# Decode attention in a paged-cache kernel: value products interleave two sequences, page numbers move ahead of a wait

## The reference, cut to what matters

```
sel_k, sel_v = sel_blocks(concat([cache_slc[page_table], new rows]))   # 1024 cached keys, 8 pages of 128 a sequence
win_k, win_v = concat([cache_win, new rows])                           # 512 cached keys
o_cmp = softmax(q . kcmp)  @ vcmp        # 32 compressed keys
o_slc = softmax(qr . kg)   @ vg          # cached keys, one block masked out
o_win = softmax(qr . win_k) @ win_v      # window keys
o = o_cmp * g0 + o_slc * g1 + o_win * g2
```

## Time and profile before

| what | value |
|---|---|
| median of three runs | 3044.95 us |
| profiled execution | 3043.31 us, its span 3041.5 us |
| PE busy | 2548.6 us (84% of the span) |
| DVE busy | 1624.8 us (53%) |
| ACT busy | 1039.4 us (34%) |
| mean TensorE clock granted | 0.877 of full speed |
| decode phase of layer 0 | from 395.7 to about 500 us |
| decode phase of layer 3 | from 2659.1 to about 2765 us |

### The profile page before, as it was taken

The page is one execution under the profiler, slowest core; times in us unless marked ns, Lnnn a source line. Parts: engine busy times, 40 slices in busy tenths (PEclk is TensorE's granted clock), DMA queues, the critical chain, the costliest instruction groups (busy, mean ns, idle before and its releaser), DMA issues. The chain is left out here.

```text
span 3041.5 us, 43305 instructions
## 1 busy us (share of the span) xinstructions
PE 2548.6 (84%) x16878; PEld 2276.5 (75%) x16878; DVE 1624.8 (53%) x2612; ACT 1039.4 (34%) x1839; POOL 126.0 (4%) x108
## 2 busy tenths in 40 slices
PE   6998677999693878786999975679999997678999
PEld 5886546999672778534999974569999885547998
DVE  4352634655546746177655665356565344635655
ACT  3221523544333111103544531145443212424543
POOL 0000000001000000000000013000010000000000
PEclk9798888999796989556999987679999797889999
DMA  5531553555230000001455430225545442372553
GB/s 210 198 97 52 180 187 112 164 165 163 95 126 21 1 1 1 32 14 51 162 166 166 146 118 0 83 87 167 165 161 171 166 135 88 107 249 87 166 165 115
DMA packets 109833, 360.70 MB, mean 119 GB/s; under 512 B 12868, under 2 KB 14660, under 8 KB 106180
## 3 DMA queue, kind: packets, MB, share of 16 engines
q1 hardware_dynamic: 107332, 353.79, 35.4%
q10 hardware_dynamic: 2304, 4.20, 0.4%
HBM read 345.97 MB, written 28.61 MB: 123 GB/s over the span
## 5 line engine op out<-in xcount | busy, mean ns | idle before, releaser
L322 DVE TENSOR_TENSOR low<-ring,high 128x1024 fp32r<-128x1024 f32 (+1 forms) x426 | 519.8, 1222 | 429.5 <-ACT high L315 429.1
L315 ACT ACTIVATE high<-ring 128x1024 fp32r<-128x1024 f32 (+1 forms) x426 | 448.6, 1056 | 653.0 <-PE bank L337 633.7
L336 PE MATMUL bank<-bl,high 128*128 128x288 f32 (+1 forms) x1616 | 482.2, 298 | 0.0
L335 PE MATMUL bank<-bh,high 128*128 128x288 f32 (+1 forms) x1616 | 479.6, 297 | 0.0
L337 PE MATMUL bank<-bh,low 128*128 128x288 f32 (+1 forms) x1616 | 474.0, 293 | 0.0
L336 PEld LDWEIGHTS bank<-bl,high 128*128 128x128 f32 (+1 forms) x1616 | 304.8, 189 | 0.8
L337 PEld LDWEIGHTS bank<-bh,low 128*128 128x128 f32 (+1 forms) x1616 | 304.5, 188 | 0.2
L336 PE MATMUL bank<-hidden_low,high 128*128 128x288 f32 x1024 | 304.5, 297 | 0.0
L335 PEld LDWEIGHTS bank<-bh,high 128*128 128x128 f32 (+1 forms) x1616 | 303.8, 188 | 0.8
L335 PE MATMUL bank<-hidden_high,high 128*128 128x288 f32 x1024 | 301.4, 294 | 0.0
L337 PE MATMUL bank<-hidden_high,low 128*128 128x288 f32 x1024 | 299.3, 292 | 0.0
(11 more groups left out here) (484 smaller groups left out, 4726.4 us busy)
## 6 DMA issues: line engine op xcount, KB each, us to landing
ring<-in_wts SPq DMA_DIRECT2D x428, 512.0 KB, 3.3
xp<-in_cmp SPq DMA_DIRECT2D x112, 256.0 KB, 3.0
raw<-in_slc SPq DMA_DIRECT2D x64, 256.0 KB, 3.6
shared<-in_slc SPq DMA_DIRECT2D x64, 256.0 KB, 3.6
out_win_out<-in_win SPq DMA_DIRECT2D x16, 1016.0 KB
raw<-in_winT SPq DMA_DIRECT2D x8, 1024.0 KB, 6.7
shared<-in_winT SPq DMA_DIRECT2D x8, 1024.0 KB, 6.7
w<-in_w SPq DMA_DIRECT2D x2, 2048.0 KB, 8.3
```

The costliest lines, as they stand in the source:

```text
L315: act.activation(ch.high[:, n % HIGHS, 0:w], ch.ring[:, q % SLOTS, 0:w], ACT.Copy).then_inc(ch.high_made, 1)
L322: dve.tensor_tensor(ch.low[:, q % SLOTS, 0:w], ch.ring[:, q % SLOTS, 0:w], ch.high[:, n % HIGHS, 0:w].bitcast(F32), ALU.subtract).then_inc ...
L335: pe.matmul(out, wh, src_h(k), start=(start and k == ks[0]), stop=False)
L336: pe.matmul(out, wh, src_l(k), start=False, stop=False)
```

## The change

There are two edits. In the products with the values PE goes over the tiles in the outer loop and over the two sequences in the inner one, so that two neighbouring instructions work for different sequences; the products with the new and compressed rows are ordered in the same manner. Their number and shapes stay. And `load_pair` reads all 16 page numbers of a pair into registers first, then waits for the buffer (where it must), then issues the two windows, and then the 16 pages.

```diff
-def load_pair(ch, sp, n_, dst, pt, bp):
-
+def load_pair(ch, sp, n_, dst, pt, bp, free=None):
+
+    pages = [[sp.value_load(pt[0:1, b * NPG + j:b * NPG + j + 1], min_val=0, max_val=79) for j in range(NPG)] for b in (2 * bp, 2 * bp + 1)]
+    if free is not None:
+        sp.wait_ge(*free)
     for b2 in range(2):
-        b = 2 * bp + b2
-        for j in range(NPG):
-            page = sp.value_load(pt[0:1, b * NPG + j:b * NPG + j + 1], min_val=0, max_val=79)
+        sp.dma_start(dst[:, b2, NPG:, :], ch.dram[f"winT{n_}"][2 * bp + b2]).then_inc(ch.pair_loaded[bp % 2], 16)
+    for b2 in range(2):
+        for j, page in enumerate(pages[b2]):
             sp.dma_start(dst[:, b2, j, :].unsqueeze(1), ch.dram[f"slc{n_}"][bass.ds(page, 1), :, :].rearrange("a p c -> p a c")).then_inc(ch.pair_loaded[bp % 2], 16)
-        sp.dma_start(dst[:, b2, NPG:, :], ch.dram[f"winT{n_}"][b]).then_inc(ch.pair_loaded[bp % 2], 16)
...
                     load_pair(ch, sp, n_, raw[1], pt, 1)
                     for bp in range(2, DB // 2):
-                        sp.wait_ge(s["pv_done"], bp - 1)
-                        load_pair(ch, sp, n_, raw[bp % 2], pt, bp)
+                        load_pair(ch, sp, n_, raw[bp % 2], pt, bp, (s["pv_done"], bp - 1))
...
-                        for b2, rows in seqs:
-                            for t in range(NPG, NT):
+                        for t in range(NPG, NT):
+                            for b2, rows in seqs:
                                 pe.matmul(win[rows, 0:2 * P], pT2[:, t, rows], kvp[:, b2, t, 2 * P:], start=(t == NPG), stop=False)
...
-                        for b2, rows in seqs:
-                            for t in range(NPG):
+                        for t in range(NPG):
+                            for b2, rows in seqs:
                                 pe.matmul(slc[rows, 0:2 * P], pT2[:, t, rows], kvp[:, b2, t, 2 * P:], start=(t == 0), stop=False)
                         pe.wait_ge(s["pt_copied"], 4 * bp + 4)
+                        for out, j in ((slc, 0), (win, 1)):
+                            for b2, rows in seqs:
+                                pe.matmul(out[rows, 0:2 * P], pTn[:, j, rows], vtok[0:NS, 2, 2 * j:2 * j + 2, :].rearrange("p a c -> p (a c)"), start=False, stop=True)
                         for b2, rows in seqs:
-                            for out, j in ((slc, 0), (win, 1)):
-                                pe.matmul(out[rows, 0:2 * P], pTn[:, j, rows], vtok[0:NS, 2, 2 * j:2 * j + 2, :].rearrange("p a c -> p (a c)"), start=False, stop=True)
                             mm = pe.matmul(cmp[rows, 2 * P:4 * P], pTn[:, 2, rows], vcs[:, 2 * bp + b2, :], start=True, stop=True)
```

## The result

The changed kernel took 3026.83 us, the median of five runs (3023.80 to 3029.56), against 3043.26 us for five runs of the kernel before. The ratio is 0.9944, with a 95% interval from 0.9929 to 0.9958. The forecast was 3029.0 us, with a range of 3020 to 3041. The profiled execution has a span of 3026.0 us, 15.5 less than before. The two decode phases, from PE's first product to the end of the last transpose, went from 104.7 and 105.7 us to 98.7 and 97.6: 14.1 of the 15.5 us are there. The other 1.4 us were gained ahead of the first of the two phases, where the change moves nothing but the reads for pair 0's load.

What follows compares the result with a forecast made beforehand. Decode phases were taken as bound by PE's chain of pairs and, beside it, SP's slowly issued loads. Three pairs' 3.65 us less pair 1's later start gave -8.05 and -7.85 us, together -15.9: 3029.0 us, range 3020 to 3041.

Steps and rivals of the forecast that it cites:

- pair 0's share: Pair 0's products with the values: their 3.65 us saving would vanish in PE's wait for pair 1's load.
- the rivals: Four alternatives: transfers gain nothing (0.13), transfers at 412 GB/s (0.15), PE stays at half clock (0.05), sequences don't overlap (0.05).
- The rival in which the transfers run as the program's first ones: Page and window loads at 412 GB/s, pair 1 landing 0.9 and 1.1 us late, whole 3025.0 us; chance 0.15.
- the signs: Expected in the trace: shorter products, PE waiting for pair 1 only, first DMA about 9 us later, clock back within products.
- The gain of a pair's products: Products with the values in the decode phases: 6.6 us against 10.25 at full clock, 3.65 us gained a pair.
- The estimate from the value of the Trainium skill for three column tiles: Products with the values: 1.59 times for two sequences, 8.3 us, gaining 1.95 a pair, whole 3039 us; not adopted.
- The landing of pair 1: Pair 1's load: 16 uncovered reads, then 20.2 us of transfer, starting pair 1 2.9 us later in layer 0, 3.1 in layer 3.
- Pairs 2 and 3: Their loads in the decode phases: reads covered, none late, with 3.5 us to spare.
- That the windows go first costs and gives nothing by itself: Window order in load_pair: worth nothing, because PE waits for all 18 DMAs.

Runs made afterwards that it cites:

- the products alone: Against the changed kernel, the loads went back to those of before while the products still alternate between the sequences: 3027.14 us, ratio 0.9944.
- windows first: Against the changed kernel, each page number is read ahead of its own page again, with the two windows still at the head of the load: 3020.61 us, ratio 0.9920.
- the clock kept: Eight products of constants per pair added while PE waits for the exponentials: 3004.36 us with windows ahead and numbers read as needed, 3016.41 us on the changed kernel.
- the loads alone: Against the changed kernel, the products went back to the order of before, with load_pair as changed: 3046.34 us, ratio 1.0007.

## Why the prediction was right, and where its terms were not

The forecast of 15.9 us less met 16.4 in the medians. Its mechanism stands: the products carry the gain (the products alone have the ratio of the full change), pair 0's share vanishes in the wait for pair 1's load, and reading numbers ahead of pair 1 costs time (3026.83 us against 3020.61 with windows first, 3016.41 against 3004.36 with the clock kept as well; with the loads alone the trace shows it, and the time doesn't). None of the rivals happened as a whole: the sequences do overlap, the clock does rise within the products, and transfers with a backlog are quicker, not as slow as before. The rival in which the transfers run as the program's first ones did happen in layer 0. Of the signs, the products (7.5 to 8.7 us a pair) and the wait ahead of pair 1 (4.0 and 5.2 us) lie partly outside what was named (6.6 to 8.3, and 5 to 8). By the terms:

- *The gain of a pair's products* was put at 3.65 us and was 2.95 as a mean of pairs 1 to 3 in both layers (11.24 before, 8.29 after). The step that failed is "The low clock at the start costs the same ... so I take 3.65 for every pair". The overlap itself is perfect, 0.216 us for two records. What is missing is the clock: the pairs in which before had it back near the start of the products (pair 2 of layer 0 and pair 3 of layer 3) begin at 1.2 GHz now like the others, and gain 1.92 and 1.69 us only. Six times 0.70 are 4.2 us less than forecast. Why the clock came back early in just these pairs is not shown: with the loads alone, which have the products of before, pairs 1 and 3 of layer 0 are quick (13 records in 2.61 and 2.51 us), and pair 2 isn't (3.98). The estimate from the value of the Trainium skill for three column tiles ("TensorE: Matmul & The Clock Gate", Part 3), 8.3 us for a pair, is met by the measured 8.29 by chance: the kernel with the clock kept takes 6.84 us with the same overlap.
- *The landing of pair 1* was put 2.9 and 3.1 us later and was 1.0 and 2.1 (27.6 and 28.5 us after the phase's first product, against 26.6 and 26.4). The reads were right: 9.5 us to the first DMA in layer 0, 9.0 in layer 3, against 9.3. The transfer was mis-sized: 20.2 us forecast, 421.93 - 403.70 = 18.2 in layer 0 and 19.5 in layer 3. With a backlog from the start the rate in layer 0 is 397 GB/s over 15 us, near the bound of the program's first loads, not the 364 of the earlier trace rows, and 18.2 us and a start 1.0 us later are what the rival with the faster transfers had for layer 0 (18.2 and 0.9). In layer 3 the transfer is only 0.7 us shorter than forecast. Both layers together give back 2.9 us.
- *The scores*, which I left alone, changed with the clock as well: pair 3 of layer 0 needs 13.05 us from its scores to its products, where before it began at full clock and needed 11.95; pair 2 of layer 3 went the other way, 11.96 against 13.05. Over the six pairs 0.2 us are gained. The turns behind the products, from the last product of a pair to the next scores or to the end of the phase, became 0.7 us longer over the six pairs (12.8 to 13.5 us); the forecast had left them as they were.
- *Pairs 2 and 3* were to find their loads landed, and did. But they also do in the kernel with windows first, which reads numbers as it goes. So reading ahead bought nothing there where it was covered, and cost where it wasn't.
- *"That the windows go first costs and gives nothing by itself"* is wrong. With numbers read as needed the windows' place is worth 6.5 us of the medians, and with the numbers in registers pair 1 starts 2.6 us earlier in the traces, both layers together, though the times can't be told apart. PE does wait for all 18; what I overlooked is that a window put last is issued after 17 paced DMAs and has its 1 MB still to move, while one put first moves while SP reads.

The 1.4 us outside the decode phases belong to no step, and nothing shows that the change made them: the kernel with the products alone has the code of before up to layer 0's decode phase, and starts it at 393.80 us in its trace, 1.9 earlier than before. Against the forecast's 15.9 us the products save 4.2 less, the landing 2.9 more and these are 1.4 more, so that they nearly cancel; the scores and the turns take another 0.5. That is why the total, 15.5 us in the spans, is closer than its parts, and it is luck.

## What to carry to other kernels

Look for matmuls that fill half of the stationary columns, and alternate the halves: two such streams ran in the time of one here, and a boundary in the old trace showed it beforehand. Before numbers are read ahead into registers, ask for each load what covers the reads; where nothing does, put the DMAs that need no register first and let them move meanwhile. When a burst of products becomes shorter, look at the clock it begins with: here filling PE's wait with products that nobody needs gave as much again as the change.

## What the runs showed of the hardware beyond that

Eight products into an unread place, 3.62 us of PE's time a pair, kept the granted clock at 1.00 through waits, transposes and products in layer 0, where the kernel without them ran at 0.50 for some 6 us (424 to 430 us in pair 1, 448 to 454 in pair 2). The kernel with them is 16 us shorter (3004.36 against 3020.61), though PE does more work.
